# Gathering a token block for 32 experts from one fp32 copy instead of three bf16 parts

## The reference, cut to what matters

```python
h = rms_norm(x2, norm_ffn_g)                    # 256 x 1024
logits = h @ router_w + router_b                # 256 x 32
top_logits, top_idx = lax.top_k(logits, 4)
gates = softmax(top_logits)
# for each expert e, over the rows xb of the tokens that chose it:
gu = xb @ w_gate_up[e] + b_gate_up[e]           # 1024 -> 2048
gate = minimum(gu[:, :1024], 7.0)
up = clip(gu[:, 1024:], -7.0, 7.0)
act = (up + 1.0) * gate * sigmoid(1.702 * gate)
y = act @ w_down[e] + b_down[e]                 # 1024 -> 1024
# y * gate value is added to the token's row; at the end rms_norm(x3, final_norm_g)
```

## Time and profile before

| | us |
|---|---|
| time, median of 3 runs (lowest to highest) | 1229.42 (1227.3 to 1230.91) |
| the profiled execution's own time | 1228.24 |
| its span in the profile | 1226.5 |
| PE busy | 1126.2 (92%) |
| PEld busy | 548.9 (45%) |
| DVE busy | 353.6 (29%) |
| ACT busy | 170.5 (14%) |
| DMA, mean over the span | 355 GB/s, 436.01 MB |

### The profile page before, as it was taken

One profiled execution on the slowest core, in us unless ns is written; L12 is line 12 of the kernel. 1 busy time (PEld: TensorE's weight loads), 2 busy tenths in 40 slices (PEclk: granted clock), 3 DMA queues, 4 the chain that ended last, 5 costly groups with the idle time before them and its releaser, 6 DMA issues.

```text
span 1226.5 us, 15442 instructions
## 1 busy us (share of the span) xinstructions
PE 1126.2 (92%) x6604; PEld 548.9 (45%) x6604; DVE 353.6 (29%) x710; ACT 170.5 (14%) x269; POOL 4.0 (0%) x23
## 2 busy tenths in 40 slices
PE   6999998987999999899899799998799998989897
PEld 5889877474343434334243334333334332434332
DVE  5683145336122212213212112212121221212213
ACT  3431233334000010101000000000000000010002
POOL 1000000000000000000000000000000000000000
PEclk9999999998999999999999999998899999989999
DMA  9731320365999999999999999999999999999994
GB/s 338 282 138 70 112 83 22 104 273 223 389 426 427 428 428 426 430 434 424 434 426 434 427 424 434 424 433 428 410 434 425 433 426 434 431 425 430 429 427 192
DMA packets 39051, 436.01 MB, mean 355 GB/s; under 512 B 5813, under 2 KB 5898, under 8 KB 20330
## 3 DMA queue, kind: packets, MB, share of 16 engines
q1 hardware_dynamic: 36938, 433.15, 84.2%
q10 hardware_dynamic: 2048, 1.86, 0.7%
HBM read 433.95 MB, written 1.05 MB: 355 GB/s over the span
## 4 chain that ended last, share of the span: by engine, by line
PE 63%; DMA 28%; DVE 3%; ACT 3%; issue 2%; SPq 0%; ACTq 0%; DVEq 0%; PEldq 0%
DMA ring<-in_w_down 22%; PE ps L1856 18%; PE ps L1896 17%; PE ps L1911 5%; PE ps L1449 4%; PE ps L1825 4%; PE ps L1502 4%; PE ps L1558 3%; DMA ring<-in_w_gate_up 3%; PE ps L1431 3%; PE ps L1554 2%; DMA work<-in_w_gate_up 2%; PE ps L1686 1%; PE ps L1730 1%; PE ps L1846 1%
## 5 line engine op out<-in xcount | busy, mean ns | idle before, releaser
L1896 PE MATMUL ps<-ring,work 128*64 128x512 f32 x1024 | 242.1, 621 | 29.8 <-DMA ring<-in_w_down 25.8
L1856 PE MATMUL ps<-work 128*64 128x512 f32 x1024 | 237.3, 607 | 3.8 <-DMA work<-in_w_gate_up 3.8
L1856 PE MATMUL ps<-ring,work 128*64 128x512 f32 x1024 | 225.5, 593 | 5.6 <-DMA ring<-in_w_gate_up 5.6
L1896 PEld LDWEIGHTS ps<-ring,work 128*64 128x64 f32 x1024 | 79.5, 142 | 167.3 <-issue 158.3
L1856 PEld LDWEIGHTS ps<-ring,work 128*64 128x64 f32 x1024 | 72.1, 137 | 153.9 <-issue 142.7
L1856 PEld LDWEIGHTS ps<-work 128*64 128x64 f32 x1024 | 74.1, 140 | 145.3 <-issue 134.1
L1331 DVE COPY work<-ps 128x512 f32<-128x512 f32 x16 | 11.1, 692 | 240.7 <-PE ps L1431 240.7
L1308 DVE TENSOR_SCALAR work<-ps 128x512 f32<-128x512 f32 x32 | 22.0, 686 | 199.0 <-PE ps L1431 199.0
L1343 DVE COPY work<-ps 128x512 f32<-128x512 f32 (+1 forms) x16 | 11.1, 691 | 208.2 <-PE ps L1896 208.2
L746 ACT ACTIVATE work<-work 128x512 f32<-128x512 f32 x32 | 20.2, 630 | 365.5 <-DVE work L1308 365.5
L1431 PEld LDWEIGHTS ps<-small,work 128*128 128x128 f32 (+1 forms) x353 | 44.0, 169 | 58.0 <-issue 53.2
(11 more groups left out here) (218 smaller groups left out, 704.9 us busy)
## 6 DMA issues: line engine op xcount, KB each, us to landing
work<-in_w_gate_up SPq DMA_DIRECT2D x64, 2048.0 KB, 28.9
ring<-in_w_gate_up SPq DMA_DIRECT2D x24, 4096.0 KB, 31.7
ring<-in_w_down SPq DMA_DIRECT2D x22, 4096.0 KB, 29.5
ring<-in_w_down SPq DMA_DIRECT2D x19, 2048.0 KB, 22.6
ring<-in_w_gate_up SPq DMA_DIRECT2D x16, 2048.0 KB, 18.0
ring<-in_w_in SPq DMA_DIRECT2D x7, 2048.0 KB, 15.6
ring<-in_xattn_w_kv SPq DMA_DIRECT2D x2, 2048.0 KB, 13.7
ring<-in_w_out SPq DMA_DIRECT2D x2, 2048.0 KB, 8.0
```

The costliest lines, as they stand in the source:

```text
L1856: last = nc.tensor.matmul(bank(b)[p], xg_T[k][:, kb, :], quad_columns(w[:, kk, :], q), start=False, stop=(kb == KB - 1))
L1896: last = nc.tensor.matmul(bank(Y_BANK + y)[p], act_T[k][:, b, HALF * c:HALF * c + HALF], w[:, b, 512 * q:512 * q + 512], start=False, stop ...
```

## The change

x2 is kept once, as it is, in fp32 (`x2_kept`, two token tiles), and the division by the root mean square goes into `pick`, which holds `rstd` instead of one and is now fp32. A gather is 8 x 2 = 16 products in fp32. The splitting of x2 is gone; ACT copies x2 to `x2_kept` in four halves. The biases are loaded once, in fp32, over three groups of 32 rows: rows 0 to 31 hold the gate biases, 32 to 63 those of up, 64 to 95 those of down; each bias product takes the 32 rows that it needs, with `choose` in fp32. Their splitting is gone too. The router's products go straight into the logits: x2_T is the stationary operand and the 32 columns of `router_w` the moving one, eight products in fp32 for a tile summed in PSUM; `move_parts` and `router_fold` are gone. For the second tile the last half of x2 goes through sum, transpose, copy and product in two quarters. The room that the parts took makes a tenth place (LONE_PLACES 6 to 9); places 6 and 7 are free to load after `moba_oT`. The gain of the final norm is loaded by SP into place 6 after its last use, rather than by ACT before the pass. Lines are left out where they only rename or move tensors.

```diff
-LONE_PLACES = [6, 7, 8]
+LONE_PLACES = [6, 7, 8, 9]
...
-FIRST_LOADS = [(0, 1), (0, 2), (0, 5), (0, 6), (0, 0), (0, 8), (0, 3), (0, 4), (0, 9)]
+FIRST_LOADS = [(0, 1), (0, 2), (0, 0), (0, 3), (0, 5), (0, 6), (0, 8), (0, 4), (0, 7), (0, 9)]
...
-        bias_raw = area(TOK, 3072)
-        bias_hi = work[:, MV:MV + 1536].bitcast(BF16)
-        bias_mid = work[:, PP:PP + 1536].bitcast(BF16)
...
+        x2_kept = area(M2, TILES, D_MODEL)
+        bias = area(QKT, D_MODEL)
+        x2_junk = area(M3 + 2560, 512)
...
+        pick = [area(MQ + P * k, TILES, SLOTS) for k in range(2)]
+        choose = area(MQ + 2 * P, 2, SLOTS)
...
+        extra = {6: area(TOK, SLOT), 7: area(M1, SLOT), 8: area(OM + 512, SLOT), 9: area(MQ + 512, SLOT)}
+        final_gain = extra[6][:, 0:D_MODEL]
+        square_junk = extra[7][:, 0:D_MODEL].rearrange("p (a b) -> p a b", b=512)
...
-                    sp.wait_ge(S("biases_ready"), 1)
-                    if s > LONE_PLACES[0]:
-                        drained(sp, "x_pv1")
+                    drained(sp, "moba_oT" if s in LONE_PLACES[0:2] else "x_pv1")
...
+            sp.wait_ge(S(f"slot_free{LONE_PLACES[0]}"), PAIRS)
+            sp.dma_start(final_gain, final_norm_g.partition_broadcast(P)).then_inc(S("final_gain_loaded"), 16)
...
-            for s in range(3):
-                act.dma_start(bias_raw[32 * s:32 * s + E, 0:2048], b_gate_up[0]).then_inc(S("bias_loaded"), 16)
-                act.dma_start(bias_raw[32 * s:32 * s + E, 2048:3072], b_down[0]).then_inc(S("bias_loaded"), 16)
+            for g in range(2):
+                act.dma_start(bias[32 * g:32 * g + E, :], b_gate_up[0, :, D_MODEL * g:D_MODEL * (g + 1)]) \
+                    .then_inc(S("bias_loaded"), 16)
+            act.dma_start(bias[64:64 + E, :], b_down[0]).then_inc(S("bias_loaded"), 16)
...
-            act.wait_ge(S("bias_loaded"), 96)
-            nc.scalar.copy(bias_hi[0:96, :], bias_raw[0:96, :]).then_inc(S("bias_high"), 1)
...
-                if t == 0:
-                    act.wait_ge(S("bias_rest"), 1)
-                    nc.scalar.copy(bias_mid[0:96, :], bias_raw[0:96, :]).then_inc(S("bias_mid"), 1)
...
-            def split_high(t):
-                act.wait_ge(S("x2_inverse"), t + 1)
-                for h in range(2):
-                    nc.scalar.activation(split[0][:, t, half_cols(h)], half_of(t, h), ACT.Copy,
-                                         scale=by_tile(rstd, t)).then_inc(S("split_high"), 1)
-            def split_mid(t):
-                for h in range(2):
-                    act.wait_ge(S("split_rest"), 2 * t + h + 1)
-                    nc.scalar.copy(split[1][:, t, half_cols(h)], remainder[:, t, half_cols(h)]) \
-                        .then_inc(S("split_mid"), 1)
+            def keep_x2(t, h):
+                nc.scalar.copy(x2_kept[:, t, half_cols(h)], half_of(t, h)).then_inc(S("x2_kept"), 1)
...
-                    v.wait_ge(S("bias_mid"), 1)
-                    nc.vector.tensor_tensor(bias_raw[0:96, :], bias_raw[0:96, :], bias_mid[0:96, :], ALU.subtract) \
-                        .then_inc(S("bias_rest"), 1)
...
-            x2_sum(0, 0)
-            x2_sum(0, 1)
+            nc.vector.memset(expert_no[0:96], 0.0).then_inc(S("expert_reset"), 1)
+            v.wait_ge(S("expert_reset"), 1)
+            v.wait_ge(S("part_no_ready"), 3)
+            choose_pair(0)
+            x2_sum(0, half_cols(0), 1)
+            x2_sum(0, half_cols(1), 0)
             x2_mean(0)
             x2_inverse(0)
-            x2_turned(0, 0)
-            x2_turned(0, 1)
-            split_rest(0, 0)
-            split_rest(0, 1)
-            x2_sum(1, 0)
-            move_parts(0)
-            split_low(0, 0)
-            split_low(0, 1)
-            x2_turned(1, 0)
+            x2_turned(0, 0, 4, 1)
+            x2_turned(0, 4, KB, 0)
+            x2_sum(1, half_cols(0), 2)
             choose_experts(0)
+            x2_turned(1, 0, 4, 2)
             x2_mean(1)
-            x2_sum(1, 1)
-            x2_turned(1, 1)
+            x2_sum(1, slice(512, 768), 3)
+            x2_sum(1, slice(768, D_MODEL), 0)
+            x2_turned(1, 4, 6, 3)
+            x2_turned(1, 6, KB, 0)
             x2_inverse(1)
-            move_parts(1)
             choose_experts(1)
-            split_rest(1, 0)
...
                     ins = nc.vector.tensor_scalar(pick[k][:, t, :], iota_s, slot_m[:, t, bass.ds(2 * i + k, 1)],
-                                                  None, ALU.is_equal)
+                                                  rstd[:, t:t + 1], ALU.is_equal, ALU.mult)
...
-                    pick_one(0, 0).then_inc(S("picked_first"), 1)
-                    split_rest(1, 1)
-                    split_low(1, 0)
-                    split_low(1, 1)
-                    pick_one(1, 0).then_inc(S("picked"), 1)
+                    pick_pair(0)
...
-            def router_parts(t):
-                name = f"logits{t}"
-                take(pe, name)
-                pe.wait_ge(S("router_gained"), 1)
-                pe.wait_ge(S("f_half_moved"), t + 1)
-                for k in range(KB):
-                    if k == 4:
-                        drained(pe, f"f_T{t}")
-                    g = 32 * (k % 4)
-                    last = nc.tensor.matmul(pair(name)[g:g + 32, 0:P], router_sb[:, k, :],
-                                            x2_T[:, k, t * P:(t + 1) * P], start=(k < 4), stop=(k >= 4))
-                last.then_inc(S("logit_parts"), 1)
-            def router_fold(t):
-                pe.wait_ge(S("logit_parts_moved"), t + 1)
-                fill_done(mm(pair(f"logits{t}")[:, 512:512 + E], logit_parts[:, t, :], fold), f"logits{t}")
+            def router_logits(t, k, k_end, n):
+                if k_end < KB:
+                    pe.wait_ge(S("f_part_moved"), n)
+                else:
+                    drained(pe, f"f_T{t}")
+                for b in range(k, k_end):
+                    last = nc.tensor.matmul(halves("logits")[:, t, 0:E], x2_T[:, b, t * P:(t + 1) * P], router_sb[:, b, :],
+                                            start=(b == 0), stop=(b == KB - 1))
+                if k_end == KB:
+                    last.then_inc(S("logits_filled"), 1)
...
-            f_turn(1, 1)
-            router_parts(1)
-            router_fold(1)
+            router_logits(1, 0, 4, 2)
+            f_turn(1, 4, 6, 3)
+            f_turn(1, 6, KB, 0)
+            router_logits(1, 4, 6, 3)
+            router_logits(1, 6, KB, 0)
...
-            def gather(k, opening=False):
+            last.then_inc(S("count_filled"), 1)
+            drained(pe, "f_T1")
+            pe.wait_ge(S("logits_moved"), TILES)
+            def gather(k):
                 dst = bank(GATHER_BANK[k])
                 for b, columns in enumerate([slice(j, 256, 2) for j in range(2)]
                                             + [slice(256 + j, 768, 4) for j in range(4)]
                                             + [slice(768 + j, 1024, 2) for j in range(2)]):
-                    if opening and b in (0, 2):
-                        pe.wait_ge(S("split_low"), TILES + 1 + b // 2)
-                    for s in range(3):
-                        for t in range(TILES):
-                            last = nc.tensor.matmul(dst[:, SLOTS * b:SLOTS * b + SLOTS],
-                                                    split[s][:, t, columns],
-                                                    pick[k][:, t, :],
-                                                    start=(s == 0 and t == 0), stop=(s == 2 and t == TILES - 1))
+                    for t in range(TILES):
+                        last = nc.tensor.matmul(dst[:, SLOTS * b:SLOTS * b + SLOTS], x2_kept[:, t, columns],
+                                                pick[k][:, t, :], start=(t == 0), stop=(t == TILES - 1))
                 last.then_inc(S("gather_filled"), 1)
...
+            bias_rows = [slice(32 * g, 32 * g + E) for g in range(3)]
             def gate_up(k, chunk, turned16, rows_gathered, between=None):
                 for q, (b, p) in enumerate(((GATE_BANK[k], low), (GATE_BANK[k], high),
                                             (UP_BANK[k], low), (UP_BANK[k], high))):
-                    nc.tensor.matmul(bank(b)[p], choose[0:96, k, :], quad_columns(bias_hi[0:96], q),
+                    rows = bias_rows[q // 2]
+                    nc.tensor.matmul(bank(b)[p], choose[rows, k, :], quad_columns(bias[rows], q % 2),
                                      start=True, stop=False)
...
-                    nc.tensor.matmul(bank(Y_BANK + y)[p], choose[0:96, k, :],
-                                     bias_hi[0:96, 2048 + 512 * q:2560 + 512 * q], start=True, stop=False)
+                    nc.tensor.matmul(bank(Y_BANK + y)[p], choose[bias_rows[2], k, :],
+                                     bias[bias_rows[2], 512 * q:512 * q + 512], start=True, stop=False)
...
+                pe.wait_ge(S("x2_kept"), 2 * TILES)
+                begin_pass(0)
```

(2 more changed lines are left out.)

251 lines of the change are left out of this document (111 added, 140 removed).

## The result

The changed kernel takes 1400.55 us (median of 4 runs, 1400.15 to 1401.24) against 1229.1 (1227.3 to 1230.91) for the kernel before in the same measurement: 1.141 times as long, 95% interval 1.139 to 1.143. The forecast was 1275 us with a range of 1262 to 1303. The direction was right, the size was not: of the 171 us that the change costs I had foreseen 46.

What follows compares the result with a forecast made beforehand. Weights bound the kernel before; the change would make TensorE the bound. Its own path of 1180.0 us plus 93.2 for gathers and biases and 0.4 start gave a 1273.6 us span, forecast 1275 us, range 1262 to 1303.

Steps and rivals of the forecast that it cites:

- What bounds the kernel: Whole pass: weights bound it, 46.5 us over TensorE's own path; up to 2.9 us a pair added to TensorE is hidden.
- The gathers: Per pair: 32 fp32 products take 7.4 us in place of 3.08 for 96 bf16 ones, +4.34 us.
- my ends, the lower: Lower end for the gathers: only moving columns count, half of 111 ns a record, 3.4 us, +0.3 a pair.
- The clock: a rival at 8%: Gathers leave the array half idle, the clock falls once a pair: +46 or +23 us, 1321 or 1298; chance 8%.
- My sign for it: Over the experts: a granted clock below 0.97 would show the forecast wrong.
- the lower case of this rival: Clock falls once a pair for half of the 6.2 us length: +23 us, 1298 us.
- Biases of gate and up: Per expert: four fp32 products run all together in 0.96 us, +0.48; ends +0.38 and +1.33.
- the rival of two at a time: Biases of gate and up: row tiles do not pair with column tiles; +26 us, 1301 us; chance 11%.
- Biases of down: Per pair: two products side by side for each expert, partly hidden by a wait, +0.69 us, between +0.4 and +0.9.
- Before the experts: Router to first gate_up: logits 0.5 us earlier, gather near 297, 5.5 us long; start shifts +0.4, between -2 and +2.
- The tenth place: 2.1 MB more weights land before the experts: 4.9 us if weights bound the pass, nothing if TensorE does.

Runs made afterwards that it cites:

- bf16_one_part: Changed kernel with x2 kept in bf16 and 96 bf16 gather products a pair, three times over the same part: 1221.85 us, ratio 0.995.
- merged_contig: Changed kernel with one gather for both experts of a pair and x2_kept stored so that loads read neighbouring columns: 1226.93 us, ratio 0.999.
- merged: Changed kernel with one gather serving both experts of a pair, 128 moving columns, columns still two and four apart: 1254.95 us, ratio 1.023.
- contig: Changed kernel with x2_kept's columns stored in the gather's reading order, so each load reads 128 neighbours: 1280.35 us, ratio 1.043.
- merged_twice: As merged, but each gather is issued twice with the same result: 1337.66 us, ratio 1.090 to the kernel before.
- best: merged_contig with the biases of down of both experts in two products instead of four, over 128 array columns: 1223.57 us, ratio 0.997.

## Why the prediction was wrong

**What bounds the kernel.** Right. TensorE had 2.9 us a pair to give by my sum; bf16_one_part used 2.06 of them at no cost, merged_contig with 2.65 was already bound by TensorE, and what went beyond was paid (merged, 4.68 us a pair over 53.25, takes 1255 us). From 364.61 us on there is no wait for weights in the changed kernel's chain. A small slip without weight in the sum: I wrote that the DMA share was 1.00 or 1.01 in every stretch, and the last of the earlier trace rows has 0.99.

**The gathers: the step that failed.** "The stretch of columns four apart has about 33 ns a product, the other 29 ... for such a slowdown on half of the products I add 0.3 us and take 7.4 us", with 8.1 as the upper end. I scaled a price of bf16 columns four apart, where the step is 8 bytes, to fp32, where it is 16, as a ratio. It is no ratio. At full clock the 32 records of each kind take 32 x 118 + 32 x 233 ns = 11.2 us, 3.8 more than my 7.4. The 222 ns for a product of neighbouring columns, from the earlier trace rows, was right (contig: 7.09 us for 32). The row that I took as "the same shape" has the same shape in the array, but another pattern in memory, and the two numbers of the earlier trace rows, 33 and 29 ns, were a warning that the pattern counts. Of my ends, the lower was also added up wrongly (64 times half of 111 ns is 3.6 us, not 3.4), which moves nothing in the forecast.

The rule of the Trainium skill that I had cited, about one 1.2 GHz cycle for each column of a load, 107 ns for 128 (TensorE: Matmul & The Clock Gate, LDWEIGHTS (loading the stationary operand), where the figure stands), agrees with contig, 111 ns a record, and differs by a factor of two from the 233 ns of columns four apart; there the measurement decides.

**The clock: a rival at 8% that held, under a price too low.** I had named the mechanism (the gathers leave the array idle once a pair) and weighed it with an array half idle and a fall of at most 6.2 us. With the loads at 233 ns it is idler than that, and the fall is 13.65 us. It costs 2.1 us in the gather (13.35 less the 11.22 that the same loads take in merged_twice at full clock), 0.9 in the biases (1.92 less 1.02) and 1.5 in gate_up (15.38 less 13.88), 4.5 us a pair. That is less than half of 13.65 us, since the 233 ns loads in it take no longer at the low clock. My sign for it came true: I had called the forecast wrong if the granted clock was below 0.97 over the experts, and it was 0.90 over the pair. I treated a dearer load and a falling clock as independent; they have one cause, and contig removes both from the second pair on. The range ended at 1303 us, where I had allowed for the lower case of this rival at my price, but for no case in which the loads cost more and the clock falls as well.

**The size of the miss.** A pair, in the sum, was forecast at 59.2 us and took 68.1. 3.8 for the loads and 4.5 for the clock are 8.3 of these 8.9; the rest is small: gate_up, whose arithmetic is unchanged, has 13.88 us of chain where it had 13.73, twice a pair (+0.3), and the biases of down are 0.2 over my term. 14 pairs by 8.9 us are 125, and 1400.6 - 1275 is 126.

**Biases of gate and up.** Right: 1.02 us in the chain where 0.57 were, +0.45 against +0.48. Their records start in fours and the rival of two at a time (+26 us) fell: row tiles and column tiles run together. TensorE in order of time, second expert:

```profile
395.78 1.09 PE L1800 MATMUL ps<-work 32*64 32x512 f32 x8
396.80 3.65 PE L1810 MATMUL ps<-work 128*64 128x512 f32 x16
```

**Biases of down.** Nearly right, within my +0.4 to +0.9. They take 1.00 us each; where the wait for ACT's copy of 0.67 us stood in the chain of before, the first now stands (+0.34), the second adds 0.68 for the 0.32 that it was; less 0.13 in the products of down behind them. +0.89 against +0.69.

**Before the experts.** Right in its sum by luck, with errors that cancel. All engines in order of time, to be laid beside the earlier trace rows:

```profile
291.43 0.25 DVE L1163 SCALAR_TENSOR_TENSOR small<-ps,small 128x32 f32<-128x32 f32 x1 [0.84 <-PE ps L1717]
...
293.31 0.23 DVE L1205 SCALAR_TENSOR_TENSOR work<-ps,small 128x64 f32<-128x64 f32 x1 [0.30 <-PE ps L1763]
...
294.49 7.36 PE L1779 MATMUL ps<-work 128*128 128x64 f32 x32 [1.17 <-DVE work L1235]
...
303.69 1.12 PE L1810 MATMUL ps<-work 128*64 128x512 f32 x2
```

The logits came 3.2 us earlier than before, not 0.5, and the gather began at 294.49, not 297; but it took 7.36 us at half clock in place of the 5.5 that I had (the clock was not back after some 4 us but at 307.8, 13.3 us after the gather began), and the first gate_up product began at 303.69 us, where I had 303.6.

**The tenth place.** Worth nothing in the changed kernel, as said; in best, where the weights bound, about 3 us, give or take 2.5, against the 4.9 worked out.

## What to carry to other kernels

Where stationary data is fp32 and read with a step, put it in the order of reading when it is written, once, and not in each load. Count loads and not only moving columns: two small products over the same stationary columns should be one. In these runs the clock then stayed at full speed even with the slow loads. Compare what an edit adds to TensorE with the slack of the whole pass and not with the weights of one pair. And when a price is carried from one row to another, compare the pattern in memory with its step in bytes as well as the shape.

## What the runs showed of the hardware that I had not expected

- An fp32 load of 128 stationary columns takes 111 ns a record for neighbours, 118 at a step of 2, 174 at 3, and 224 to 238 from 4 to 8.
- The 233 ns of step 4 do not depend on the granted clock (they are the same at 1.2 and 2.4 GHz), while the step of 2 goes from 118 to 213 ns.
- A gather of steps 2 and 4 with 64 moving columns, 11.2 us long at full clock, brought the clock down once in each pair, for 13.65 us in most; the same loads with 128 moving columns did not, nor did 14.2 us of fast loads with 64. Where the clock was low already, fast loads with 64 moving columns left it low (17.07 and 20.48 us against 3.41 to 6.83 with 128).
- A short product in front of a wait is partly free: with 0.94 us of biases of down less, a pair became 0.58 us shorter.
